# Output projection of a hybrid trunk layer: the first weight chunk split into its high and low halves inside the attention, in buffers of its own

## The reference, cut to what matters

```python
mod = silu(cond) @ w_ada + b_ada                       # six vectors: sh1, sc1, g1, sh2, sc2, g2
h = rms_norm(x, norm_mix) * (1 + sc1) + sh1
q, k, v, conv_in, pool_in, four_in = split(h @ w_in)
attn = softmax(q k^T / 8) v                            # 8 query heads, 2 key heads; latent queries also see 128 cached keys
conv = silu(layer_norm(depthwise_conv31(a * sigmoid(gate))))
pool = (window_mean(pool_in) - pool_in) @ pool_w * pool_scale
four = real(fft2(four_in))
x = x + g1 * (concat(attn, conv, pool, four) @ w_out)  # w_out is 2048 x 1024: the output projection
h = rms_norm(x, norm_ffn) * (1 + sc2) + sh2
x = x + g2 * moe(h)                                    # 4 groups of 4 experts, 2 of one group for each token
y = rms_norm(x, final_norm)
```

## Time and profile before

| | |
|---|---|
| median of 3 runs | 703.83 us |
| lowest and highest of them | 702.86 and 706.41 us |
| the profiled execution: its time | 707.6 us |
| its span in the trace | 705.2 us |
| mean granted clock of TensorE in it | 0.944 of full |
| TensorE busy | 606.4 us (86% of the span) |
| VectorE busy | 532.2 us (75%) |
| ScalarE busy | 336.2 us (48%) |
| GpSimd busy | 140.2 us (20%) |

### The profile page before, as it was taken

The page is one execution under the profiler, slowest core; times in us unless marked ns, Lnnn a source line. Parts: engine busy times, 40 slices in busy tenths (PEclk is TensorE's granted clock), DMA queues, the critical chain, the costliest instruction groups (busy, mean ns, idle before and its releaser), DMA issues.

```text
span 705.2 us, 8279 instructions
## 1 busy us (share of the span) xinstructions
PE 606.4 (86%) x3212; PEld 483.0 (68%) x3212; DVE 532.2 (75%) x670; ACT 336.2 (48%) x446; POOL 140.2 (20%) x96
## 2 busy tenths in 40 slices
PE   0879999999999979999799999934999999999540
PEld 0269778899888656556578888824888887878430
DVE  0583599999999777998863520797999988888487
ACT  5143124331113645556645311363588887877542
POOL 0002000006994000000222432011132312221300
PEclk9989999999999989999999999975999999999865
DMA  7972955555002100000344400097799999997663
GB/s 274 413 266 97 348 179 179 185 201 207 12 2 86 59 0 1 1 0 1 120 145 164 150 1 1 0 363 300 266 381 396 387 362 362 379 350 281 225 275 149
DMA packets 44190, 133.44 MB, mean 189 GB/s; under 512 B 9328, under 2 KB 18132, under 8 KB 36472
## 3 DMA queue, kind: packets, MB, share of 16 engines
q1 hardware_dynamic: 36552, 121.49, 46.2%
q0 software_dynamic: 5184, 10.50, 3.9%
q10 hardware_dynamic: 2416, 0.92, 0.5%
HBM read 126.96 MB, written 14.32 MB: 200 GB/s over the span
## 4 chain that ended last, share of the span: by engine, by line
PE 47%; DVE 28%; DMA 17%; issue 3%; ACT 3%; SPq 1%; POOL 0%; ACTq 0%; DVEq 0%; POOLq 0%
DMA m_raw<-in_moe_w_down_dram 9%; DVE cy L1482 9%; PE ps L574 7%; PE ps L576 7%; PE ps L575 7%; DMA raw<-in_w_ada_dram 4%; PE ps L738 3%; PE ps L875 2%; PE ps L878 2%; PE ps L877 2%; DVE w_lo L1440 2%; PE ps L556 2%; DMA yb<-y_rows 1%; PE ps L865 1%; DVE ss_qk L1597 1%
## 5 line engine op out<-in xcount | busy, mean ns | idle before, releaser
L1482 DVE SCALAR_TENSOR_TENSOR cy<-cu,tapw,cy 128x655 f32<-128x655 f32 x120 | 114.7, 956 | 3.5
L1900 DVE TENSOR_TENSOR gu_lo<-m_raw,gu_hi 128x2048 fp32r<-128x2048 f32 x36 | 82.2, 2289 | 8.1 <-ACT gu_hi L1202 6.6
L1202 ACT ACTIVATE gu_hi<-m_raw 128x2048 fp32r<-128x2048 f32 x36 | 68.9, 1919 | 17.2 <-DMA m_raw<-in_moe_w_gate_dram 8.7
L875 PE MATMUL ps<-gu_hi,xt_h 128*128 128x512 f32 x144 | 60.3, 419 | 7.6 <-DVE gu_lo L1900 7.6
L1353 POOL TENSOR_TENSOR w_lo<-raw,w_hi 128x2048 fp32r<-128x2048 f32 x7 | 32.7, 4677 | 166.0 <-ACT w_hi L1130 166.0
L574 PE MATMUL ps<-w_hi,mix 128*128 128x512 f32 x160 | 62.9, 393 | 2.8 <-DVE w_lo L1679 2.8
L877 PEld LDWEIGHTS ps<-gu_lo,xt_h 128*128 128x128 f32 x288 | 56.3, 195 | 12.6
L576 PE MATMUL ps<-w_hi,mix 128*128 128x512 f32 x160 | 62.4, 390 | 0.0
L575 PE MATMUL ps<-w_lo,mix 128*128 128x512 f32 x160 | 62.3, 390 | 0.0
L878 PE MATMUL ps<-gu_hi,xt_l 128*128 128x512 f32 x144 | 58.5, 406 | 0.0
L877 PE MATMUL ps<-gu_lo,xt_h 128*128 128x256 f32 x288 | 58.4, 285 | 0.0
(11 more groups left out here) (351 smaller groups left out, 1426.7 us busy)
## 6 DMA issues: line engine op xcount, KB each, us to landing
raw<-in_w_ada_dram SPq DMA_DIRECT2D x24, 1024.0 KB, 7.5
m_raw<-in_moe_w_gate_dram SPq DMA_DIRECT2D x18, 1024.0 KB, 9.7
m_raw<-in_moe_w_up_dram SPq DMA_DIRECT2D x18, 1024.0 KB, 12.8
m_raw<-in_moe_w_down_dram SPq DMA_DIRECT2D x18, 1024.0 KB, 14.8
raw<-in_w_in_dram SPq DMA_DIRECT2D x11, 1024.0 KB, 7.1
raw<-in_w_out_dram SPq DMA_DIRECT2D x8, 1024.0 KB, 5.6
h_rows<-h2k SPq DMA_DIRECT2D x5, 512.0 KB, 12.0
ya<-y_rows SPq DMA_DIRECT2D x5, 512.0 KB, 7.6
```

Of the source, the lines that this page charges most:

```text
L875: pe.matmul(out, xt_h[q][:, k, :], gu_hi[q][:, k, :], start=(k == 0), stop=False)
L1202: act.activation(gu_hi[q][:, :, u * FF:(u + 1) * FF], m_raw[3 * s + u][:, :].rearrange("p (k n) -> p k n", k=KB), ACT.Copy).then_inc((g_hi ...
L1482: ins = dve.scalar_tensor_tensor(out=cy[:, blk, :], in0=cu[:, blk, i:i + CY], scalar=w, in1=cy[:, blk, :], op0=MUL, op1=ADD)
L1900: dve.tensor_tensor(gu_lo[s][u][:, :, :], m_raw[3 * s + u][:, :].rearrange("p (k n) -> p k n", k=KB), gu_hi[q][:, :, u * FF:(u + 1) * FF]. ...
```

## The change

The halves of chunk 0 get buffers of their own, `wo_first`. The high half lies at `L`, over the queries in `qkv`: its 8,192 bytes cover the rows of token tiles 0 and 1 and the queries of tile 2. The low half lies over raw chunk 0 itself, so the subtraction works in place. ScalarE copies the high half in four pieces of 512 columns, each right after `probs(u, 3)` of units 4 to 7. The first piece waits for the chunk and for the last read of the latent and context queries (`qs_lo` 9; VectorE's `queries_lo(7)` stands at the head of its unit 4). VectorE subtracts in unit 8, ahead of `inverse(3, 0)`. `wo_split(0)` and the subtraction after the units go away. Chunk 0 on TensorE reads `wo_first`; chunk 2 no longer waits for TensorE's end of chunk 0, since `w_hi[0]` had no user before it. Chunk 4, which falls into the raw buffer where the low half of chunk 0 now lies, waits for TensorE's end of chunk 0 (`wo_used` 1).

```diff
+    wo_first = at("wo_first_hi", [CHUNK], L, f32r), at("wo_first_lo", [CHUNK], RAW + 8192 * WO_SLOT[0], f32r)
...
         def w_out_chunk(i):
             n, cc, s = i // 4, WO_PART[i % 4], WO_SLOT[i % 4]
-            if i >= NRAW:
+            if i == NRAW:
+                sp.wait_ge(wo_used, 1)
+            elif i > NRAW:
                 sp.wait_ge(wo_lo, i - NRAW + 1)
...
             pe.wait_ge(wo_lo, i + 1)
-            hi = w_hi[i % 2][:, :].rearrange("p (k n) -> p k n", k=4)
-            lo = w_lo[i % 2][:, :].rearrange("p (k n) -> p k n", k=4)
+            hi, lo = (w[:, :].rearrange("p (k n) -> p k n", k=4) for w in (wo_first if i == 0 else (w_hi[i % 2], w_lo[i % 2])))
...
+        def first_wo_piece(n):
+            if n == 0:
+                wait_raw(act, "w_out", 0)
+                act.wait_ge(qs_lo, HEADS + 1)
+            piece = slice(n * CHUNK // 4, (n + 1) * CHUNK // 4)
+            ins = act.activation(wo_first[0][:, piece], raw[WO_SLOT[0]][:, piece], ACT.Copy)
+            if n == 3:
+                ins.then_inc(wo_hi, 1)
...
             for kt in range(2, n_keys(u)):
                 probs(u, kt)
+                if kt == 3 and 4 <= u < HEADS:
+                    first_wo_piece(u - 4)
...
         def wo_split(i):
             wait_raw(act, "w_out", i)
-            if i == 0:
-                act.wait_ge(st_ps, key_count(UNITS, 0))
             if i == 1:
                 act.wait_ge(pv_step, key_count(UNITS, 0))
-            if i >= 2:
+            if i >= 3:
                 j = i - 2
...
-        wo_split(0)
         take_out(UNITS - 2)
         take_out(UNITS - 1)
...
                 row_max(u + 2, 0)
+            if u == UNITS - 2:
+                dve.wait_ge(wo_hi, 1)
+                dve.tensor_tensor(wo_first[1][:, :], raw[WO_SLOT[0]][:, :], wo_first[0][:, :].bitcast(f32), SUB).then_inc(wo_lo, 1)
             if e >= 0:
                 inverse(e, 0)
...
-        dve.wait_ge(wo_hi, 1)
-        dve.wait_ge(pv_step, key_count(UNITS, 0))
-        dve.tensor_tensor(w_lo[0][:, :], raw[WO_SLOT[0]][:, :], w_hi[0][:, :].bitcast(f32), SUB).then_inc(wo_lo, 1)
         normal(3)
```

## The result

| | kernel before | changed kernel |
|---|---|---|
| median of 22 runs each, on the same chips | 707.07 us | 704.92 us |
| lowest and highest | 702.86 and 709.83 us | 702.13 and 707.35 us |
| ratio, 95% interval | | 0.9962 (0.9947 to 0.9976) |
| the profiled execution: time, span | 707.6, 705.2 us | 705.94, 703.9 us |

The change makes the kernel faster by 0.38% (0.24 to 0.53), that is 2.7 us (1.7 to 3.7). The recorded ratio is not that of the two medians, which differ by 2.15 us. The forecast change of 2.0 us lies within that; the forecast time does not hold. 704.92 us is above the range of 699.9 to 704.3, because the kernel before itself measures 707.07 us in 22 runs and not the 703.83 us of the three that the forecast started from.

What follows compares the result with a forecast made beforehand. VectorE's series, beside TensorE's chunk 0, was taken to bound the second sum of channels; -2.14 + 0.1 = -2.0 us, subtracted from the 703.83 us median, gave 701.8 us, range 699.9 to 704.3.

Steps and rivals of the forecast that it cites:

- The sum: VectorE's series ahead of TensorE's second sum of channels: -2.14 + 0.1 = -2.0 us, everything behind moving by 2.0 us.
- The subtraction's removal: On VectorE behind the units, chunk 0's low-half subtraction goes: -2.14 us.
- The term for its new place: VectorE's subtraction in unit 8, ahead of the reciprocals, mostly covered by the wait for ScalarE: +0.1 us.
- What bounds: From 341 to 358 us VectorE's series ends 0.22 us behind TensorE's chunk 0; TensorE's earlier 2.76 us rest isn't the price.
- The rest that comes back: TensorE's wait for VectorE ahead of the second sum of channels: 1.0 us of the old rests of 2.98 us.
- The cap of 2.98 us: TensorE's rests ahead of chunk 0 and the second sum, 2.76 + 0.22 us, taken as the limit of any gain.
- The costs at nothing: ScalarE's four pieces in units 4 to 7, its removed copy, and the changed waits: each costed at 0.
- SyncE's new wait: Chunk 4 waits for TensorE's end of chunk 0, about 355.7 us; SyncE stands until 362.07 us anyway: 0.
- The held instruction: Faster rival, chance 0.12: GpSimd's lock holds `mix` instead of VectorE's fourth mean subtraction, gaining 0.76 us more, 701.1 us.
- Lost behind: Rival, chance 0.10: the experts' stage is bound by transfers that don't start earlier, so no change, 703.8 us.
- Attention ends later than 340.57 us (pieces on the path): Sign that the forecast is wrong: attention's end moves later because ScalarE's pieces delay it.
- the slower rival: Chance 0.08: ScalarE's pieces in units 4 to 7 land on the path, up to 2.5 us, giving 704.3 us.

Runs made afterwards that it cites:

- the repetition: The changed kernel run again beside the kernel before: ratio 0.9973 (0.9948 to 0.9999); 16.32 us from TensorE's first sum of channels to its second.
- The late low half: Changed kernel with VectorE's low half of chunk 0 back behind the units, only the high half in pieces: ratio 0.9991 against the kernel before.
- Chunk 1 on VectorE, in both kernels: Low half of chunk 1 made by VectorE instead of GpSimd: ratio against the kernel before 0.9949 in the changed kernel, 0.9990 in the kernel before.
- the kernel against itself: The kernel before submitted unchanged as if it were a changed one: ratio 0.9993 (0.9965 to 1.0021), median 707.28 us of 12 runs.
- One piece: Changed kernel with chunk 0's high half as one copy of 2048 columns in unit 4, not four pieces: ratio 0.9957 against the kernel before.
- more copies: Changed kernel with a second ScalarE copy of 384 columns ahead of each of the four pieces: ratio 0.9958 against the kernel before.

## Why the prediction was right or wrong

**The sum: right.** VectorE's series was to get 2.0 us shorter; sum to sum is 1.81 us shorter in the two executions and 1.83 in the repetition (18.15 - 16.32). Both terms were a little off. The subtraction's removal was to give -2.14 and gave -2.03: from the start of the reciprocals to `normal(3)` it is 3.39 us (344.05 - 340.66) instead of 5.42 (344.45 - 339.03), because the instruction behind the reciprocals used to follow them at 3.28 us and now follows at 3.39. The term for its new place was +0.1; it is +0.19, of which 0.06 are its own length (2.29 us instead of 2.23, in place). The late low half shows that the whole of it hangs on that one move.

**What bounds: right.** The 2.76 us were not the price. The rest that comes back was to be 1.0 us and is 1.45: TensorE starts chunk 0 at 1.01 us behind the start of the sum of channels, not 1.27 (matmuls overlap), and VectorE is 0.2 us later than forecast. This changes nothing in the sum, as VectorE's series sets the second sum. Chunk 1 on VectorE, in both kernels, shows the two series as forecast. The cap of 2.98 us, which gave the range its lower end, was too low: 3.43 us were reached.

**The costs at nothing: right.** Pieces of 0.62 us under waits of 1.59 to 0.74 us leave 1.10 to 0.21 us. SyncE's new wait is not felt: chunks 3 to 5 are sent for at 361.68 us, right behind `am_lo` 6, in one group of three.

```profile
361.68 1.49 SPq L414 DMA_DIRECT2D raw<-in_w_out_dram  x3
```

**The held instruction: right as to its cause, as a rival not met.** The fourth subtraction takes 5.251 us in the changed kernel, as before, since GpSimd starts at the same distance behind the first (347.35 - 345.52 = 1.83 us, before 1.82). With GpSimd idle it takes 0.84.

```profile
L1696 DVE TENSOR_TENSOR cy<-cy,ln_v x4: 835/840/5251, 345.5 to 347.8; 128x655 f32<-128x655 f32 x4
```

My price for the rival was too high: if GpSimd began 0.5 us later it would also end 0.5 us later, and of the 0.76 us at most 0.3 would stay. That GpSimd starts later was not tried.

**Lost behind: not met.** From the second sum to the experts' first request nothing is lost (99.11 and 99.09 us); what the experts' stage adds or takes scatters by 2 us over the ten traces, with the change and without.

**A sign of being wrong that misled.** "Attention ends later than 340.57 us (pieces on the path)" came true in the profiled execution (341.99), and for another reason, the clock from 260 to 265 us. An absolute time holds everything ahead of it; the distance from unit 4 was the right sign, and it didn't move.

**The time and its range: wrong.** The step that failed is the last of the sum, its base: "This execution lies 3.8 us above the median of 703.83, so I subtract from the median: 701.8 us", and then the range. Its upper end, 704.3, is the slower rival's price on that same median with nothing for the scatter of the base; its lower end takes "about 1 us, the distance of the median from the lowest of three runs" for it. With the 22 runs the median of before is 707.07 us, 3.2 us higher, and 2.0 less than that is 705.1. The profiled execution at 707.6 us was the ordinary one, and the three runs were low. Subtracting 2.0 us from 707.6 gave 705.6, which stood in the working and is 0.7 us from the measured 704.92. Two of those three runs (703.83 and 702.86) lie below all 82 runs of before that the experiments brought (lowest 704.47), and below the 19 others of the result (lowest 704.62). Whether the three came from a faster chip or hour or from chance is open; the kernel against itself showed no difference within one chip. A range in microseconds had to hold that scatter of the base, about 3 us either way, on top of the bounds of the change. The forecast of the change held: the prediction gave 0.77 to a change of less than 0.5%, and 0.38% was measured.

**Left open.** The ratio of the 22 runs says 2.7 us, the traces 1.8. The interval (1.7 to 3.7 us) holds both, the medians differ by 2.15, and the repetition gives 0.9973, 1.9 us. One piece and more copies, which differ from the changed kernel by 0.1 us at most in their stages, gave 0.9957 and 0.9958, intervals to 0.9982. Up to the experts' stage the traces leave no room for a further gain: ahead of and behind the 1.81 us the distances from unit 4's query subtraction on are the same in both kernels (37.05 and 37.04, then 99.11 and 99.09 us). Behind it, a gain below 1 us can't be told from the scatter of 2 us there. No experiment names one.

## What to carry to other kernels

When one engine waits 2.8 us for another, look at what the other does behind that: here the rest of VectorE's series was as long as TensorE's, and only what left it was gained. Before moving work off VectorE, see what holds it: one GpSimd instruction beside it cost 4.4 us, twice as much as taking that work over. Carry a change as a difference, and take the base from many runs: three runs of a kernel that scatters by 7 us or more fix it no better than a few microseconds.

## What the runs showed of the hardware

**An instruction of VectorE with two SBUF operands waits for a whole instruction of GpSimd, not for a share of bandwidth.** A subtraction of two SBUF operands takes 0.84 us alone, 5.25 us when it starts 0.46 us behind a GpSimd instruction of 4.99 us, and 1.38 us when GpSimd's work comes in eight parts. In that last kernel (timeline of VectorE) the other two-operand instructions are lengthened too, `mix` from 0.68 to 1.23 us and the three of `csq` from 2.59 to 3.96, while the reciprocals, with one operand, keep their 1.75 us in the midst of it:

```profile
346.92 1.23 DVE L1653 TENSOR_TENSOR mix<-cx,mix 128x512 fp32r<-128x512 f32 x1
348.07 1.75 DVE L1638 RECIPROCAL dnp<-dnp 128x128 f32<-128x128 f32 x2
...
350.34 3.96 DVE L1707 TENSOR_TENSOR csq<-csq 128x655 f32<-128x655 f32 x3
```

The Trainium skill states it so (SBUF — State Buffer, "SBUF: two separate sides"): an instruction of VectorE with two SBUF inputs and one of GpSimd that reads SBUF exclude each other, and the second waits for the whole of the first. By that rule, these traces agree. The wait works both ways: GpSimd's eight parts take 8.43 us instead of 4.99. Each takes from 0.73 to 1.34 us, the shortest while VectorE is at its reciprocals. Eight of the shortest would be 5.9 us (an estimate), so about 2.5 us of the 8.43 are waiting and the rest of the growth is the price of eight instructions in place of one.

```profile
L1366 POOL TENSOR_TENSOR w_lo<-raw,w_hi x8: 732/1150/1339, 345.2 to 352.3; 128x256 fp32r<-128x256 f32 x8
```

**The moment at which TensorE's clock comes back scatters.** From 255 to 260 us it is granted 0.50 to 0.75 in every trace, behind a stretch (250 to 255 us) with TensorE busy for 3.5 to 3.6 of 5 us. From 260 to 265 us it is 0.86 to 0.99 in seven traces and 0.50 in three (the changed kernel, the late low half, more copies). The row maxima from the first to the last take 63.8 to 64.9 us in the seven and 66.3 in the three. One such draw is worth 1.4 us or more, nearly as much as the change.
